# Silu of the gated networks: one ScalarE Silu in place of a tanh and a VectorE product

## The reference, cut to what matters

```
def swiglu(h, w_gate, w_up, w_down):                      # ff1, ff2: 2816 hidden columns
    return (jax.nn.silu(h @ w_gate) * (h @ w_up)) @ w_down

def conv_glu_ffn(u, w_up, conv_w, conv_b, w_down):        # glu1, glu2: 3072 hidden columns
    gu = u @ w_up
    gate = causal_dwconv(gu[..., :D_FF_2], conv_w) + conv_b
    return (jax.nn.silu(gate) * gu[..., D_FF_2:]) @ w_down
```

## Time and profile before

| | |
|---|---|
| median of 3 runs | 1331.43 us (1328.64 to 1332.31) |
| the profiled execution: its time, its span | 1332.08 us, 1330.3 us |
| TensorE matmul busy | 1304.7 us, 98% of the span |
| VectorE, ScalarE, GpSimd busy | 978.6 us (74%), 684.7 us (51%), 97.4 us (7%) |
| mean granted TensorE clock | 0.995 of full speed |
| HBM | 161 GB/s over the span |

### The profile page before, as it was taken

How to read it: one execution, slowest core, us unless ns; L and a number is a source line. 1 busy time by engine, 2 the same in 40 slices (tenths; PEclk the granted TensorE clock), 3 DMA queues, 4 the chain that set the end, 5 groups by cost and what they waited for, 6 DMA issues and landing times.

```text
span 1330.3 us, 23126 instructions
## 1 busy us (share of the span) xinstructions
PE 1304.7 (98%) x9032; PEld 1186.6 (89%) x9032; DVE 978.6 (74%) x1547; ACT 684.7 (51%) x1073; POOL 97.4 (7%) x93
## 2 busy tenths in 40 slices
PE   7999999999999999999999999999999999999998
PEld 6888889998888888988999999899998888999997
DVE  6866777767687666786776666899896965766665
ACT  5444455666554444765554444677542545544442
POOL 1000000000000000220000000014001820000000
PEclk9999999999999999999999999999997999999999
DMA  8655545720455555404455555444430124655551
GB/s 304 214 205 189 189 158 175 257 92 1 143 202 208 189 189 190 159 33 159 141 208 189 187 179 187 143 161 161 155 127 33 65 95 132 218 190 189 189 190 64
DMA packets 30601, 214.83 MB, mean 161 GB/s; under 512 B 3648, under 2 KB 3776, under 8 KB 5184
## 3 DMA queue, kind: packets, MB, share of 16 engines
q1 hardware_dynamic: 30096, 212.23, 45.6%
q0 software_dynamic: 432, 1.57, 0.4%
HBM read 212.74 MB, written 1.05 MB: 161 GB/s over the span
## 4 chain that ended last, share of the span: by engine, by line
PE 85%; DVE 9%; ACT 2%; issue 2%; DMA 1%; POOL 0%; SPq 0%; POOLq 0%; DVEq 0%; ACTq 0%
PE bank L503 32%; PE bank L508 25%; PE bank L675 12%; PE bank L712 5%; DVE w_lo L2198 2%; PE bank L891 1%; PE bank L496 1%; PE bank L941 1%; PE bank L910 1%; ACT w_hi L1485 1%; DVE arena L2817 1%; DVE par L2815 1%; DVE aT L2432 1%; PE bank L561 1%; DMA raw<-weights 1%
## 5 line engine op out<-in xcount | busy, mean ns | idle before, releaser
L2198 DVE TENSOR_TENSOR w_lo<-raw,w_hi 128x2048 fp32r<-128x2048 f32 x194 | 447.4, 2307 | 160.9 <-ACT w_hi L1485 160.6
L1485 ACT ACTIVATE w_hi<-raw 128x2048 fp32r<-128x2048 f32 x198 | 377.8, 1909 | 81.5 <-PE bank L712 46.5
L503 PE MATMUL bank<-aT,w_hi 128*128 128x256 f32 x1952 | 245.6, 284 | 0.0
L503 PEld LDWEIGHTS bank<-aT,w_hi 128*128 128x128 f32 x1952 | 239.7, 192 | 1.6
L508 PE MATMUL bank<-aT,w_lo 128*128 128x256 f32 x1664 | 216.3, 283 | 0.0
L508 PEld LDWEIGHTS bank<-aT,w_lo 128*128 128x128 f32 x1664 | 209.7, 192 | 3.4
L675 PE MATMUL bank<-aT,w_hi 128*128 128x512 f32 x688 | 164.8, 391 | 0.8 <-DVE aT L2225 0.7
L1555 ACT ACTIVATE arena<-arena 128x256 f32<-128x256 f32 x92 | 38.4, 418 | 230.3 <-DVE arena L2483 150.1
L503 PE MATMUL bank<-w_hi,hT_hi 128*128 128x512 f32 x400 | 156.5, 391 | 0.0
L508 PE MATMUL bank<-w_lo,hT_hi 128*128 128x512 f32 x400 | 151.9, 389 | 0.0
L675 PEld LDWEIGHTS bank<-aT,w_hi 128*128 128x128 f32 x688 | 127.2, 188 | 27.5 <-DVE aT L2225 1.4
(11 more groups left out here) (388 smaller groups left out, 1579.2 us busy)
## 6 DMA issues: line engine op xcount, KB each, us to landing
raw<-weights SPq DMA_DIRECT2D x198, 1024.0 KB, 4.9
post_gain<-post_gains POOLq DMA_DIRECT2D x3, 512.0 KB, 5.0
residual<-x SPq DMA_DIRECT2D x2, 512.0 KB, 4.1
raw<-weights SPq DMA_DIRECT2D x2, 512.0 KB, 7.2
out<-residual SPq DMA_DIRECT2D x2, 512.0 KB, 2.6
par<-params SPq DMA_DIRECT2D x1, 809.0 KB, 11.3
con<-consts SPq DMA_DIRECT2D x1, 520.0 KB, 11.0
con<-consts SPq DMA_DIRECT2D x1, 64.0 KB, 4.2
```

The source lines that it names most:

```text
L503: nc.tensor.matmul(to, lhsT, rhs, start=start and n == 0, stop=False)
L1485: nc.scalar.activation(w_hi[:, i % 3, :], raw[:, i % 3, :], ACT.Copy).then_inc(w_hi_done, 1)
L2198: nc.vector.tensor_tensor(w_lo[:, i % 3, :], raw[:, i % 3, :], w_hi[:, i % 3, :].bitcast(f32), ALU.subtract).then_inc(w_lo_done, 1)
```

## The change

In the four networks the tanh with scale 0.5 becomes a Silu with no scale, and the VectorE instruction (tanh + 1) * gate goes away with its semaphore. The remaining VectorE product is `f_silu` * up, a tensor_tensor instead of a scalar_tensor_tensor, and waits for the Silu directly. The silu of the delta rule layer (lines 1833, 1891, 2779) stays as it was. In VectorE's code lines behind this place move up by five.

```
@@ ScalarE, the gated networks' tile
-                    nc.scalar.activation(f_tanh[:, f % 2, :], tanh_of, ACT.Tanh, scale=0.5).then_inc(gate_tanh, 1)
+                    nc.scalar.activation(f_silu[:, f % 2, :], silu_of, ACT.Silu).then_inc(gate_silu, 1)
@@ VectorE, the gated networks' tile
-                    dve.wait_ge(gate_tanh, f0 + f + 1 + 4 * q)
-
-                    nc.vector.scalar_tensor_tensor(f_tanh[:, f % 2, :], f_tanh[:, f % 2, :], 1.0, gate,
-                                                   ALU.add, ALU.mult).then_inc(silu_step, 1)
-                    dve.wait_ge(silu_step, f0 + f + 1 + 4 * q)
+                    dve.wait_ge(gate_silu, f0 + f + 1 + 4 * q)
                     if not conv:
                         dve.wait_ge(up_sum, (f0 and 22) + f + 1 + 4 * q)
-                    nc.vector.scalar_tensor_tensor(f_hid[:, f % 2, :], f_tanh[:, f % 2, :], 0.5, up,
-                                                   ALU.mult, ALU.mult).then_inc(hid_ready, 1)
+                    nc.vector.tensor_tensor(f_hid[:, f % 2, :], f_silu[:, f % 2, :], up, ALU.mult).then_inc(hid_ready, 1)
```

More of the change, by code:

```diff
@@ L156, in two_blocks @@
         f_gate = room(2, SEQ)
-        f_tanh = room(2, SEQ)
+        f_silu = room(2, SEQ)
         f_hid = room(2, SEQ)
@@ L285, in two_blocks @@
         gate_sum, up_sum = sem("gate_sum"), sem("up_sum")
-        gate_scaled, gate_conv, gate_tanh = sem("gate_scaled"), sem("gate_conv"), sem("gate_tanh")
+        gate_scaled, gate_conv, gate_silu = sem("gate_scaled"), sem("gate_conv"), sem("gate_silu")
         hid_ready, hid_hi, hid_lo = sem("hid_ready"), sem("hid_hi"), sem("hid_lo")
@@ L291, in two_blocks @@
         half_turned, half_hi, half_lo = sem("half_turned"), sem("half_hi"), sem("half_lo")
-        y_squares, conv_step, silu_step = sem("y_squares"), sem("conv_step"), sem("silu_step")
+        y_squares, conv_step = sem("y_squares"), sem("conv_step")
         setup_hi, setup_done = sem("setup_hi"), sem("setup_done")
@@ L1543, in tile @@
                         act.wait_ge(gate_sum, (f0 and 22) + f + 1 + 4 * q)
-                        tanh_of = f_gate[:, f % 2, :]
+                        silu_of = f_gate[:, f % 2, :]
                     if conv:
```

## The result

The changed kernel takes 1333.44 us (median of 17 runs, 1331.53 to 1335.18) beside 1330.59 us (17 runs, 1328.26 to 1332.34) of the kernel before on the same chip: ratio 1.0023, 95% interval [1.0016, 1.003], 2.85 us more. In microseconds the interval runs from 2.1 to 4.0. The forecast was +2.8 us, 1334.2 us. The profiled execution took 1334.65 us, with a span of 1332.8 us and a mean granted clock of 0.994.

The account below looks back on a forecast made before the run. TensorE, busy 98% of the span, was taken to bound the kernel. Two exposed table loads, 1.42 + 1.40 = +2.8 us, other terms 0, gave 1334.2 us against the median; the 8 in 10 range was 1330.0 to 1339.0 us.

Parts of the forecast that it names:

- TensorE has no wait in the networks, so VectorE's saving is worth 0: Gated networks: removing 92 VectorE instructions, 38.7 us, gains TensorE 0; bounds 0 and 3.1 us.
- Silu at 418 ns, 15 loads of 1.28 us, ScalarE at 697.5 us: Signs of being right on ScalarE: Silu costs what Tanh did, 15 loads of 1.28 us, busy time near 697 us.
- Ten loads hidden: Ten of twelve loads fall in ScalarE's idle time or where TensorE has no wait: 0; 14.2 us without cover.
- `att_in` +1.42 us: Load ahead of the Exp at 578.28 has no idle and delays TensorE: +1.42 us, bounds 0 and 2.8.
- `gdn_qkv` +1.40 us: Load at k = 2, line 1884, has no idle and reaches TensorE's line 1145 at k = 8: +1.40 us, bounds 0 and 2.8.
- The hard step: In `gdn_qkv`, VectorE works without a pause until 917.03, so it doesn't win back the 1.40 us.
- All hidden: Rival: ScalarE is idle half the time, so no TensorE wait grows, 1331.4 us; chance 0.15.
- only `att_in`: Rival: VectorE or ScalarE wins back the `gdn_qkv` 1.40 us between 874 and 903 us, 1332.8 us; chance 0.15.
- faster: Rival: VectorE's shorter order starts the seams between networks earlier and loads cost nothing, 1328.3 us; chance 0.05.
- Double price: Rival: each exposed switch costs two load lengths as ScalarE empties and fills, 5.4 us, 1336.8 us; chance 0.05.
- The clock case: Rival: TensorE's longer pause in `att_in` drops its clock, losing 3.2 to 6.5 us, 1337 to 1341 us; chance 0.10.
- a clock below 1.00 behind 581 us: Sign of being wrong: TensorE's granted clock below 1.00 after 581 us, in `att_in`.

Follow-up runs that it names:

- e1: Kernel before with its tanh kept and the VectorE product (tanh + 1) * gate left out, no load added: 1330.5 us, ratio 0.9995.
- e8: Changed kernel with one-column Exps moving both exposed loads early, plus four unread filler matmuls among the delta rule's first products: 1327.7 us, ratio 0.998.
- e9: Kernel before with four unread filler matmuls in the delta rule and nothing else: 1327.63 us, ratio 0.9983.
- e11: Changed kernel with both loads early and six fillers, four in the delta rule's first products, one in `att_in`, one ahead of `inv_T_64(0, 0)`: 1326.88 us, ratio 0.9972.
- e12: Kernel before with six unread filler matmuls, one in `att_in` and the others in the delta rule, on another chip: 1326.77 us, ratio 0.9977.
- e4: Changed kernel with one-column Exps in both `att_in` and `gdn_qkv`, so both exposed loads stand in ScalarE's idle time: 1331.5 us, ratio 1.0007.
- e5: Kernel before, tanh and both products kept, with a one-column Silu ahead of the last block copy of `att_in`: 1332.61 us, ratio 1.0012.
- e2: Changed kernel with a one-column Exp ahead of the last block copy of `att_in`, so that load comes early: 1331.34 us.
- e6: Kernel before, tanh and both products kept, with a one-column Silu at the first block of `gdn_qkv`: 1330.81 us, ratio 1.0006.
- e3: Changed kernel with a one-column Exp at k = 0 of `gdn_qkv`, so only that load comes early: 1333.31 us.
- e7: Changed kernel with three unread 128x512 matmuls in TensorE's pause in `att_in`: 1334.39 us, ratio 1.0027.
- e10: Changed kernel, both loads left exposed, with four unread filler matmuls in the delta rule: 1330.79 us, ratio 1.0005.

## Why the prediction was right, point by point

- **TensorE has no wait in the networks, so VectorE's saving is worth 0.** Right in what counts: the rows do have two short waits at tile lines (675 and 503, both for `aT`, the input of a layer), but none for what the change touches. The saving is worth nothing by e1, e8 against e9, e11 against e12. VectorE's busy time was mis-sized: 943.3 us and not 939.9 us. The working took 92 x 421 ns = 38.7 us off, but the page's busy time is a union, and an instruction starts before its neighbour has ended; taking one out frees 35.3 / 92 = 384 ns.
- **Silu at 418 ns, 15 loads of 1.28 us, ScalarE at 697.5 us.** Measured 418 ns, 15 loads, 698.0 us.
- **Ten loads hidden.** Right: the starts table has no loss at them, and at line 1718 the first exponential is 0.3 us late against the copies ahead of it (276.56 after 276.05 us, less the 0.2 us of the start) and the second is on time, as worked out. With the other two moved early (e4), TensorE's waits are those of the kernel before but for the one at line 675, and the time is 0.9 us above it or less.
- **`att_in` +1.42 us.** Right in mechanism and size: the pause grew by 1.42 us (1.16 to 2.58), and e5 makes it with one column of Silu.
- **`gdn_qkv` +1.40 us.** Right: a new wait of 1.42 us at line 1145, released by line 1877. The hard step, that VectorE never catches up over 30 us, held; e2 and e6 measured 1.1 to 1.7 us at one clock.
- **All hidden, only `att_in`, faster.** All three fall: the loss is clear of noise, e6 prices the second load by itself, and e1 finds no gain at the seams.
- **Double price.** Wrong, as the forecast had it: the exponential starts 0.02 us behind the load, and the two waits grew by one load each. Nothing like the 1380 ns of drain of the Trainium skill, "ScalarE: Activation LUTs", section "What ACT_TABLE_LOAD costs", shows at either load.
- **The clock case.** Held at 0.10 and as an alternative to the forecast; it came on top of it. A fall to 0.50 from 584 to 591 us follows the pause of 2.58 us in the profiled execution, and e3's runs at 0.992 suggest the same. The prediction had listed a clock below 1.00 behind 581 us as a sign that it was wrong, and this sign came. What the prediction missed is that the fall in the delta rule has no fixed length: in the traces it lasted 13.7 us (before, e2 to e7), 10.2 us (e1) and 6.8 us (after), and the shorter one of after gave 2.9 us back. The step that failed is "1334.2 + 3.2 to 6.5 = 1337 to 1341 us", which added the new fall to an old one taken as fixed, and took it for half of the delta rule's or more. Whether the first fall shortens the second is not settled: in the profile after 6.8 us in `att_in` go with 6.8 us in the delta rule, in e5's 3.4 us go with the full 13.7.
- **How much is luck.** The two loads at 2.8 us are not: e9 and e10 find 3.1 us at a clock of 1.000, and the four runs of the changed kernel at 0.997 (mean 1331.8 us) are 2.8 to 3.2 us above before's groups at that clock in the other sets. That the medians agree with the forecast to 0.05 us is luck: the interval runs from 2.1 to 4.0 us, the clock falls come and go from run to run, and the forecast had no term for them.

## What to carry to other kernels

A table load costs its 1.3 us only where ScalarE has no idle time ahead of the instruction and an engine that sets the end waits behind it. So walk the new loads one by one, and move an exposed one with a one-column call into an earlier idle stretch. Where a mean clock stands beside each run, compare runs at one clock before believing a difference of 2 us in the medians; e6 and e7 both mislead by their medians. Count the clocks too, since a change can shift them, as the load in `att_in` seems to do. And look at a short stretch of low clock behind a few waits before looking at the work in it: six matmuls that nobody reads won 3.4 to 3.6 us here, and 92 removed instructions nothing.

## What the runs showed of the hardware that was not expected

- Fillers of 0.70 and 1.02 us (as e8's trace has them) at the short waits (0.5 to 1.1 us) kept the granted clock at 1.00 through the delta rule in the traces of e8, e10, e11 and e12, where before it was at 0.50 for 13 us although TensorE was busy 12.47 of them. With four of them e9's trace still has 6.8 us at 0.50. Six are worth 3.6 us in the medians (e12, 1326.77 us, beside 1330.41 us of before).
- A load placed at the head of a hardware loop is executed in each iteration, though its set is active from the second one on: four of the 8 loads at line 1555. Here they cost nothing.
- Most of the kernel's spread from run to run, 4 us, goes with the clock: with six fillers, at 0.999 to 1.000, it is 0.7 us.
